# Two transformer blocks on one core: each 512-column product of the first down projection issued as two of 256

## The reference

```
x = x + mixed @ w_out
x = x + conv_glu(rms_norm(x, norm2_g), w_ffn_up, ffn_conv_w, ffn_conv_b, w_ffn_down)

def conv_glu(x, w_up, conv_w, conv_b, w_down):
    hid = x @ w_up                      # 512 x 5632
    hid = conv(hid, conv_w) + conv_b    # three taps along the tokens
    gate, up = hid[..., :D_FF], hid[..., D_FF:]
    return (silu(gate) * up) @ w_down   # 512 x 2816 by 2816 x 1024: the first down projection
```

## Time and profile before

| | |
|---|---|
| median of three runs | 1734.41 us |
| the profiled execution | 1730.57 us |
| its span (first to last instruction) | 1728.8 us |
| TensorE, matmuls | 1695.1 us busy, 98% of the span |
| TensorE, weight loads | 1344.1 us busy, 78% |
| VectorE, ScalarE, GpSimd | 34%, 39%, 44% |
| granted TensorE clock, mean | 0.998 |
| memory traffic | 84 GB/s |

### The profile page before, as it was taken

How to read it: one execution, slowest core, us unless ns; L and a number is a source line. 1 busy time by engine, 2 the same in 40 slices (tenths; PEclk the granted TensorE clock), 3 DMA queues, 4 the chain that set the end, 5 groups by cost and what they waited for, 6 DMA issues and landing times.

```text
span 1728.8 us, 22714 instructions
## 1 busy us (share of the span) xinstructions
PE 1695.1 (98%) x7752; PEld 1344.1 (78%) x7752; DVE 594.4 (34%) x963; ACT 666.8 (39%) x1151; POOL 767.7 (44%) x605
## 2 busy tenths in 40 slices
PE   7999999999999999999999999999999999999998
PEld 5776777677788888888678877777777888888877
DVE  4055513324343333300466432554423111110144
ACT  5233364233354444422443434523334333332342
POOL 7444432224364444444567423222346444444442
PEclk9999999999999999999999999999999999999999
DMA  4421121112243333323222223221223333333312
GB/s 150 122 87 49 50 74 56 49 55 83 65 116 98 97 97 97 98 97 94 78 74 74 68 61 110 67 56 49 80 79 103 96 95 96 101 106 98 93 56 95
DMA packets 103208, 145.58 MB, mean 84 GB/s; under 512 B 11094, under 2 KB 56895, under 8 KB 102991
## 3 DMA queue, kind: packets, MB, share of 16 engines
q1 hardware_dynamic: 102958, 142.30, 27.7%
q10 hardware_dynamic: 160, 2.11, 0.3%
HBM read 142.24 MB, written 2.13 MB: 84 GB/s over the span
## 4 chain that ended last, share of the span: by engine, by line
PE 89%; DVE 4%; ACT 3%; issue 2%; POOL 2%; DMA 1%; SPq 0%; DVEq 0%; ACTq 0%
PE bank L1484 76%; PE bank L1427 4%; PE bank L1404 3%; PE bank L1412 1%; DVE work L1320 1%; PE bank L1609 1%; POOL w_lo L617 1%; PE bank L1582 1%; ACT L799 1%; POOL h_lo L467 1%; DMA w_raw<-in_w_in 1%; ACT h_hi L859 0%; DVE h_lo L467 0%; PE bank L1630 0%; DMA xtok<-in_x 0%
## 5 line engine op out<-in xcount | busy, mean ns | idle before, releaser
L617 POOL TENSOR_TENSOR w_lo<-w_raw,w_hi 128x512 fp32r<-128x512 f32 x516 | 682.2, 1330 | 809.5 <-ACT w_hi L792 806.8
L792 ACT ACTIVATE w_hi<-w_raw 128x512 fp32r<-128x512 f32 x516 | 318.8, 629 | 675.6 <-PE bank L1484 599.3
L1484 PE MATMUL bank<-h_hi,w_lo 128*128 128x512 f32 x1376 | 550.4, 400 | 7.3 <-ACT hk L882 2.8
L1484 PE MATMUL bank<-h_hi,w_hi 128*128 128x512 f32 x1376 | 537.4, 391 | 0.0
L1484 PE MATMUL bank<-h_lo,w_hi 128*128 128x512 f32 x1376 | 537.1, 390 | 0.0
L1484 PEld LDWEIGHTS bank<-h_hi,w_lo 128*128 128x128 f32 x1376 | 259.0, 188 | 90.7 <-issue 22.9
L1484 PEld LDWEIGHTS bank<-h_hi,w_hi 128*128 128x128 f32 x1376 | 258.8, 188 | 55.2
L1484 PEld LDWEIGHTS bank<-h_lo,w_hi 128*128 128x128 f32 x1376 | 259.3, 188 | 54.1 <-issue 2.9
L1484 PE MATMUL bank<-g_hi,w_lo 128*128 128x512 f32 x352 | 137.0, 389 | 0.0
L1484 PE MATMUL bank<-g_hi,w_hi 128*128 128x512 f32 x352 | 136.9, 389 | 0.0
L1484 PE MATMUL bank<-g_lo,w_hi 128*128 128x512 f32 x352 | 136.9, 389 | 0.0
(11 more groups left out here) (262 smaller groups left out, 1765.8 us busy)
## 6 DMA issues: line engine op xcount, KB each, us to landing
w_raw<-in_w_in SPq DMA_DIRECT2D x168, 256.0 KB
w_raw<-in_w_ffn_up SPq DMA_DIRECT2D x88, 256.0 KB
w_raw<-in_w_ffn_down SPq DMA_DIRECT2D x88, 256.0 KB
w_raw<-in_w_ffn_gate SPq DMA_DIRECT2D x88, 128.0 KB
w_raw<-in_w_ffn_up SPq DMA_DIRECT2D x88, 128.0 KB
w_raw<-in_w_out SPq DMA_DIRECT2D x32, 256.0 KB
w_raw<-in_w_branch_b SPq DMA_DIRECT2D x16, 256.0 KB
w_raw<-in_w_branch_a SPq DMA_DIRECT2D x16, 256.0 KB
```

What stands on the lines that cost most here:

```text
L617: e.tensor_tensor(w_lo[:, pos % SPLIT_SLOTS, :], w_raw[:, pos % RAW_SLOTS, :], w_hi[:, pos % SPLIT_SLOTS, :].bitcast(F32), ALU.subtract).t ...
L792: e.activation(w_hi[:, pos % SPLIT_SLOTS, :], w_raw[:, r, :], ACT.Copy).then_inc(hi_full, 1)
L1484: mm = e.matmul(ps[banks + n][:, :], l, r, start=k == 0 and i == 0, stop=k == p.kc - 1 and i == 2)
```

## The change

In the phase `down1`, each of the three products of a tile is issued as two matmuls: one of the token columns 0 to 255, one of the columns 256 to 511. Both have the same 128x128 weights, and write their own half of the bank. The first product of a tile carries the flag that starts a sum, and now both its halves do. The second down projection and all other phases keep products of 512.

```diff
                 else:
                     ops = [(w_lo[:, pos, c], x_hi), (w_hi[:, pos, c], x_lo), (w_hi[:, pos, c], x_hi)]
+                if name == "down1":
+                    for i, (l, r) in enumerate(ops):
+                        for t in (slice(0, S // 2), slice(S // 2, S)):
+                            mm = e.matmul(ps[banks + n][:, t], l, r[:, t], start=k == 0 and i == 0,
+                                          stop=k == p.kc - 1 and i == 2, skip_group_check=True)
+                    return mm
                 for i, (l, r) in enumerate(ops):
                     mm = e.matmul(ps[banks + n][:, :], l, r, start=k == 0 and i == 0, stop=k == p.kc - 1 and i == 2)
                 return mm
```

## The result

Eleven runs of each kernel were timed: the changed kernel takes 1740.39 us (median, 1737.39 to 1742.8), the kernel before 1732.77 us (1730.46 to 1735.12). The ratio is 1.0043, with a 95% interval of 1.0033 to 1.0052. That is 5.7 to 9.0 us slower; the forecast was 7.1 us, a ratio of 1.0041. The profiled execution took 1737.39 us with a span of 1735.7, where 1737.7 and 1735.9 were forecast.

What follows compares the result with a forecast made beforehand. TensorE, busy 98% of the span, was taken as the bound; columns and hidden loads add nothing, 528 extra seams of 13.4 ns add 7.1 us, so 1734.4 + 7.1 = 1741.5 us, range 1733 to 1751.

Steps and rivals of the forecast that it cites:

- The path: down1's 528 products, 119.68 us with TensorE always busy, pass any change into the end time one for one.
- The columns: In down1, 512 columns at one per 2.4 GHz clock take 213.3 ns of the 226.7 ns per product.
- The weight load costs nothing: In down1 the added weight loads hide behind the stream of the half in front, so they cost nothing.
- The bound of 109 ns: Plain 128-column passes, each with a full load, start every 109 ns; a half of down1 can't come faster.
- rival B: In down1 halves go at the pace of the loads, 109 ns each: -4.6 us, 1729.8 us; chance 0.04.
- Rival D: In down1 the second load isn't hidden, 0.107 us for each half: 113 us on top, 1854 us; chance 0.06.
- The seam comes twice: The 13.4 ns beside a down1 product's stream belong to each product, so a pair costs +13.4 ns: +7.1 us; chance 0.50.
- Rival A: In down1 the rest goes with the columns; the added seam costs 0.5 to 1.6 us, 1735 to 1736; chance 0.18.
- Rival C: In down1 the distances between products stay uneven, +24.0 ns a pair: +12.7 us, 1747.1 us; chance 0.18.
- The products with eight weight columns: Rows with an 88 ns load instead of 188 come at 230 ns, taken as showing the rest isn't paid for loading.
- particular to this format: Plain 512-column passes show a seam of 1 to 3 ns, so down1's 13.4 ns were laid to its product format.
- the unevenness behind a pause: From 369.80 to 370.96 five distances average 232 ns and are uneven, taken as a cost between products, not of columns.

## Why the prediction was right

*The path.* The stretch was said to lie on the path with nothing beside or behind it to take the change up. Right: the phase grew by 7.03 us, the last pieces of the chain stand 6.85 us later, and the second down projection, issued in halves too, costs 120.0 ns for a half as well.

*The columns.* 213.3 ns of stream was my reading of one column a clock. The widths 512, 384 and 256 give 53.3 ns for 128 columns, which shows it.

*The weight load costs nothing.* Right for the halves. The prediction saw their cover as exactly used up, 106.7 ns of stream for a load that needs as long. In fact they come every 120.0 ns, and the floor is at 111.6. The bound of 109 ns from the run of 32 narrow passes was 2.6 ns too low; its first load started 0.22 us ahead of its product, which may be the reason. Of rival B that leaves even less. Rival D is refuted by the trace, where the products of the stretch start 0.12 us apart:

```profile
711.93 0.40 PE L1486 MATMUL bank<-g_hi,w_lo 128*128 128x256 f32 x2
712.17 0.40 PE L1486 MATMUL bank<-g_lo,w_hi 128*128 128x256 f32 x2
712.41 0.40 PE L1486 MATMUL bank<-g_hi,w_hi 128*128 128x256 f32 x2
```

A row holds the two halves of a product, 0.24 us from the next.

*The seam comes twice.* Right, in sign, place and size: 13.3 ns measured for each product at three widths, 13.4 put down. Rival A (the rest goes with the columns) asked for halves 113 ns apart and 170 ns for 384 columns, and is ruled out by 120.0 and 173.4. Rival C (the seam stays uneven, 125 ns) is ruled out by the 120.0 ns of both halved phases.

*What I argued for it was weaker than the result.* Two of the supports don't carry. The products with eight weight columns were to show that "the rest is not paid for loading weights": with 32 columns it is 2.2 ns less in halves and 5 ns more in whole products, so the load isn't without a part. The 13.4 ns were said to be "particular to this format": 16-bit numbers read with the same step of 4 bytes have 11.7 ns at 512 columns. The third, the unevenness behind a pause, which spoke for a cost between products, was tested by no run. What did carry was taking the size from the rows of the very phase. That all of the 13.4 ns would come twice was thus a choice that the rows before hardly supported, and some luck is in it: with every second 16-bit number as operand, 11.7 ns beside the stream looked much the same at 512 columns, and a pair would have cost 1.7 ns more and not 13.4.

*The range.* Its upper end doesn't follow from its own terms: rival C and 2 us for scatter give 1747.1 + 2 = 1749 us, and not 1751. The measured 1740.39 us lies inside either.

*Open.* Where the 13.3 ns arise. What lies beside the stream changed with the format, with the step of the streamed operand and with the width of the weights: with rounded 32-bit numbers and full loads the seam is fixed; with every second 16-bit number it goes mostly with columns; with neighbours it is 2.5 ns.

## What to carry to other kernels

Where TensorE is the bound without a gap, count products as well as columns. In this kernel each product of rounded 32-bit numbers with full weight loads cost its columns at 2.4 GHz and 13.3 ns, so the widest piece, 512 columns, was the cheapest. Below about 236 columns the columns and the seam fall under 111.6 ns (an estimate from these two figures: 98.3 ns of stream). A narrower piece still costs about 112 ns, as those of 192 and of 128 columns did, and narrowing it saves nothing. To tell a cost of a product from a cost of its columns, measure a third width. When two sums share a bank, mind that the flag that starts the second one drops what the first has summed up.

## What the runs showed of the hardware that I had not expected

- A product of rounded 32-bit numbers with only 128 columns stays in one pass (111.6 ns a piece, against 218 for two narrow plain passes).
- Fewer weight columns can make wide products slower: 231.7 ns with 32 of them, 226.7 with 128.
- The rest beside the stream differs with the operand: at 512 columns it is 2.5 ns for neighbouring 16-bit numbers of a constant tile, 11.7 for every second one of the activations, and 13.3 for rounded 32-bit ones. Whether the step or the constant values make the first difference was not separated.
- The flag that starts a sum in one half of a bank drops what the other half has summed up, though it writes none of its columns: a result off by 0.3202, as the reference is without those products.
